# Hybrid decoder step: the rows of u and of v are fetched by two gathers in two layouts

## The chip, the cores and the metric

The kernel runs on one core of a Trainium2 chip, as one program. The metric is the device time of one execution in microseconds (us); a run's figure is the median of its executions. Five engines work beside each other and meet at semaphores: PE (TensorE, matrix products), DVE (VectorE), ACT (ScalarE), POOL (GpSimd) and SP (SyncE, which here only issues DMAs). Indirect DMAs, which fetch rows by a list of indices, are issued by POOL.

## The reference

One layer: a mixer (convolution and gated linear attention), then PEER, a retrieval of single-neuron experts. Only PEER is touched by the change. It runs over 1088 tokens (1024 of a prompt and 64 of samples):

```python
s = einsum('thpd,hpkd->thpk', (h @ wq), subkeys)       # 8 heads, 2 halves, 128 keys
sv, si = top_k(s, 16)
cand, cand_id = 16 x 16 sums of the two halves, ids si0 * 128 + si1
top_v, top_i = top_k(cand, 16)                         # 8 heads x 16 = 128 picks of a token
expert = cand_id[top_i]; gate = softmax(top_v)
act = gelu(einsum('thkd,td->thk', u_tab[expert], h))   # u_tab: 16384 x 1024
out = einsum('thk,thkd->td', gate * act, v_tab[expert])  # v_tab: 16384 x 1024
```

Each token picks 128 experts. For every pick a row of u (4 KB in float32) is needed for the dot product with the token's h, and a row of v (4 KB) is added to the token's output with the weight gate * gelu(dot).

## The kernel before

The program is a row of phases, one after the other: conditioning, attention heads, convolution, gates, merge, output projection, keys (which writes the lists `best` and `place`), then `gather_phase` (PEER proper) and `final_phase` (last norm and residual). The change is in `gather_phase` alone, and in `arrange`, which lays out the tables.

`gather_phase` takes the tokens in nine tiles: eight of 128 tokens and one of 64 (`NT`, `rows`). In each tile it goes token by token, in the order of `token_order` (column c of each of four groups of 32 tokens, then the next column), and makes batches of four tokens (`BT`).

- **POOL** issues one indirect DMA for each token (L1361). The 128 partitions hold the 128 picks of that token, the table `uv` has u and v side by side, so each of the 128 rows is 8 KB and a DMA brings 1 MB. There are `NUV` = 11 buffers of 1 MB. Before a DMA, POOL waits until the v product of the batch that used the buffer has been done (`v_mm`).
- **PE** spreads the token's h over all 128 partitions (`spread`, L1402: two products of 96 x 512 in bf16, h being held as three bf16 pieces, selected by `sel`), two tokens ahead at most (PSUM banks 0 to 3). It also makes the weighted sum of v rows (`gathered`, L1416), one batch behind: for each token two float32 products with a weight column `zw` into banks 4 and 5.
- **DVE** multiplies the token's u rows by the spread h and adds up along the row (L1632, one custom instruction with a u buffer in SBUF and the spread h in PSUM as its inputs), then, once per batch, makes gate * gelu in `weigh` (L1611). Four times in a tile it does a part of the next tile's choice of experts (`pick`, L1555 to L1592).
- **ACT** does gelu once per batch (L1529), cuts h into its bf16 pieces (L1470 to L1479), copies the turned h out of PSUM (L1487), and takes the finished tile out of PSUM and back (`emptied`, `returned`).
- **SP** loads h of the next tile and stores the output of the last.

The order on each engine is written out by hand in these loops. Waits are semaphores; an engine works its instructions strictly in the order in which they stand, so whatever stands behind a waiting instruction waits too. The lines that the change touches:

## Time and profile before

| | |
|---|---|
| median of 3 runs | 4817.19 us (4813.33 to 4823.47) |
| the profiled execution's own time | 4813.56 us |
| its span | 4811.8 us |
| first to last indirect DMA of `gather_phase` | 1883.91 to 4723.17 us, 1088 of them |
| busy share of the span: PE, DVE, POOL, ACT | 68%, 49%, 29%, 11% |
| queue of the indirect DMAs | 1140.92 MB, 57.5% of the 16 DMA engines' time over the whole span |

A span is the time from the first to the last instruction of the profiled execution; what lies around it is 1.8 us. A line of a profile view names the kernel's line, the engine, the operation, what is written <- what is read, shapes, count; then busy time, mean duration in ns, and the idle time that the engine had just before such instructions with who ended it. The share in which the 16 DMA engines are busy, and what they move, is a line of its own. "PEclk" is TensorE's granted clock as a share of its full speed.

### The profile page before, as it was taken

How to read it: one execution, taken by the hardware profiler on the slowest of the kernel's cores; microseconds unless marked ns; L12 is line 12 of the kernel's file. 1: busy time of each engine (PE TensorE's matmuls, PEld its weight loads, DVE VectorE, ACT ScalarE, POOL GpSimd, SP SyncE). 2: the span in 40 equal slices, each digit the busy share in tenths (PEclk: the TensorE clock that was granted, in tenths of full speed). 3: DMA queues.
4: the chain of work that ended last, by engine and by line, in shares of the span. 5: the costliest groups of instructions: out<-in, count | busy, mean ns of one | idle time of the engine just before them, and what ended most of it. 6: DMA issues, size and time to landing. Idle time of an engine off the chain costs nothing. (4 is left out here: it accounts for less than half of the span.)

```text
span 4811.8 us, 43674 instructions
## 1 busy us (share of the span) xinstructions
PE 3292.1 (68%) x15775; PEld 1751.6 (36%) x15775; DVE 2358.9 (49%) x5057; ACT 551.5 (11%) x999; POOL 1412.9 (29%) x1297
## 2 busy tenths in 40 slices
PE   8688996988984992566665665565665666655674
PEld 2577885988983990111111111111111111111111
DVE  0355335300314676655555555556546555556543
ACT  1222222011013111000000000000000000000001
POOL 0311100222311111343433333433333434333330
PEclk9899998999997995666666666666666766666687
DMA  6110111022321104999999999999999999999996
GB/s 247 48 46 27 46 38 55 26 95 111 124 87 77 54 22 183 396 392 410 409 388 409 393 405 408 385 422 401 388 421 405 391 406 411 390 406 411 417 422 251
DMA packets 206836, 1302.03 MB, mean 271 GB/s; under 512 B 25537, under 2 KB 42561, under 8 KB 61266
## 3 DMA queue, kind: packets, MB, share of 16 engines
q0 software_dynamic: 156672, 1140.92, 57.5%
q1 hardware_dynamic: 47554, 140.09, 8.0%
q10 hardware_dynamic: 2448, 18.88, 1.0%
q8 instruction: 100, 1.64, 0.1%
q14 instruction: 62, 0.51, 0.0%
HBM read 1259.27 MB, written 40.54 MB: 270 GB/s over the span
## 5 line engine op out<-in xcount | busy, mean ns | idle before, releaser
L1632 DVE CUSTOM_DVE_ANT_0 peer_uv<-peer_uv,all_PS 128x1024 f32<-128x1024 f32 x1088 | 1313.1, 1220 | 1245.7 <-PE all_PS L1402 694.7
L1361 POOL DMA_INDIRECT peer_uv<-in_uv,peer_idx x1088 | 1052.6, 967 | 1778.9 <-PE all_PS L1416 1493.0
L1416 PE MATMUL all_PS<-peer_uv,peer_zw 128*32 128x512 f32 x4352 | 947.8, 982 | 583.7 <-DVE peer_zw L1611 579.2
L1402 PE MATMUL all_PS<-peer_hT,peer_sel 96*128 96x512 bf16 x2176 | 770.2, 467 | 441.5 <-DVE peer_dots L1632 439.7
L1402 PEld LDWEIGHTS all_PS<-peer_hT,peer_sel 96*128 96x128 bf16 x2176 | 167.3, 107 | 1245.5 <-DVE peer_dots L1632 759.8
L1416 PEld LDWEIGHTS all_PS<-peer_uv,peer_zw 128*32 128x32 f32 x4352 | 165.3, 152 | 1136.2 <-DVE peer_zw L1611 762.8
L1529 ACT ACTIVATE peer_ge<-peer_dots 128x4 f32<-128x4 f32 x272 | 56.1, 206 | 2631.6 <-DVE peer_dots L1632 2626.7
L124 PE MATMUL all_PS<-stream_h_hi,keys_w_hi 128*128 128x384 f32 (+1 forms) x384 | 127.2, 331 | 60.3 <-DVE keys_w_lo L1239 51.4
L133 POOL CAST gla_w_hi<-gla_w 128x1024 fp32r<-128x1024 f32 x24 | 27.7, 1153 | 426.6 <-DMA gla_w<-in_w_heads 273.5
L124 PE MATMUL all_PS<-stream_h_hi,side_w_hi 128*128 128x384 f32 (+1 forms) x384 | 126.4, 329 | 16.8 <-DVE side_w_lo L771 16.8
L124 PE MATMUL all_PS<-stream_h_hi,gla_w_hi 128*128 128x384 f32 (+1 forms) x384 | 126.0, 328 | 1.8 <-DVE gla_low L641 1.8
L125 PE MATMUL all_PS<-stream_h_lo,side_w_hi 128*128 128x384 f32 (+1 forms) x384 | 126.2, 329 | 0.0
L126 PE MATMUL all_PS<-stream_h_hi,side_w_lo 128*128 128x384 f32 (+1 forms) x384 | 126.2, 329 | 0.0
L126 PE MATMUL all_PS<-stream_h_hi,keys_w_lo 128*128 128x384 f32 (+1 forms) x384 | 126.1, 328 | 0.0
L125 PE MATMUL all_PS<-stream_h_lo,keys_w_hi 128*128 128x384 f32 (+1 forms) x384 | 126.1, 328 | 0.0
L126 PE MATMUL all_PS<-stream_h_hi,gla_w_lo 128*128 128x384 f32 (+1 forms) x384 | 125.2, 326 | 0.0
L125 PE MATMUL all_PS<-stream_h_lo,gla_w_hi 128*128 128x384 f32 (+1 forms) x384 | 125.1, 326 | 0.0
L124 PE MATMUL all_PS<-stream_h_hi,conv_w_hi 128*128 128x384 f32 (+1 forms) x288 | 95.7, 332 | 23.8 <-DVE conv_w_lo L771 23.8
L771 DVE TENSOR_TENSOR merge_w_lo<-merge_w,merge_w_hi 128x512 fp32r<-128x512 f32 (+1 forms) x2 | 1.9, 958 | 201.3 <-ACT merge_w_hi L764 201.3
L124 PEld LDWEIGHTS all_PS<-stream_h_hi,keys_w_hi 128*128 128x128 f32 x384 | 72.9, 190 | 62.5 <-issue 51.9
L125 PE MATMUL all_PS<-stream_h_lo,conv_w_hi 128*128 128x384 f32 (+1 forms) x288 | 95.6, 332 | 0.0
L126 PE MATMUL all_PS<-stream_h_hi,conv_w_lo 128*128 128x384 f32 (+1 forms) x288 | 95.5, 331 | 0.0
(293 smaller groups left out, 4960.7 us busy)
## 6 DMA issues: line engine op xcount, KB each, us to landing
cond_w<-in_w_ada SPq DMA_DIRECT2D x12, 2048.0 KB, 7.7
peer_uv<-in_uv,peer_idx POOLq DMA_INDIRECT x1088
gla_w<-in_w_heads SPq DMA_DIRECT2D x24, 512.0 KB, 3.3
scratch_sig<-side_sig ACTq DMA_DIRECT2D x8, 1088.0 KB, 4.0
merge_sig<-scratch_sig ACTq DMA_DIRECT2D x8, 1088.0 KB, 5.0
side_w<-in_w_gate_ab SPq DMA_DIRECT2D x16, 512.0 KB, 3.2
keys_w<-in_w_query SPq DMA_DIRECT2D x16, 512.0 KB, 3.2
conv_w<-in_w_conv SPq DMA_DIRECT2D x12, 512.0 KB, 3.2
```

Of the source, the lines that this page charges most:

```text
L124: nc.tensor.matmul(bank[:, 0:n], w_hi[:, k, :], hi, start=(k == 0), stop=False)
L125: nc.tensor.matmul(bank[:, 0:n], w_hi[:, k, :], lo, start=False, stop=False)
L126: last = nc.tensor.matmul(bank[:, 0:n], w_lo[:, k, :], hi, start=False, stop=(k == nk - 1))
L133: nc.gpsimd.tensor_copy(hi, raw).then_inc(high, 1)
L771: nc.vector.tensor_tensor(self.lo[:, b, 0:nk], self.raw[:, b, 0:nk], self.hi[:, b, 0:nk].bitcast(F32), ALU.subtract).then_inc(self.low, 1)
L1361: nc.gpsimd.indirect_dma_start(out=uv[:, n % NUV, :], out_offset=None, in_=A["uv"], in_offset=bass.IndirectOffsetOnAxis(ap=idx[:, t % 2, r ...
L1402: last = nc.tensor.matmul(PS[:, 2 * (n % 2) + e, :], sel[:, c, :], hT[:, t % 2, j, e * 512:(e + 1) * 512], start=True, stop=True)
L1416: last = nc.tensor.matmul(PS[j * GR:(j + 1) * GR, 4 + e, :], zw[:, z, GR - 1 - c:2 * GR - 1 - c], uv[:, n % NUV, D + e * 512:D + (e + 1) * ...
L1529: nc.scalar.activation(ge[:, n % ND, :], dots[:, n % ND, :], ACT.Gelu_apprx_tanh).then_inc(M["gelled"], 1)
L1632: nc.vector.tensor_tensor_reduce(u, u, PS[:, 2 * (n % 2):2 * (n % 2) + 2, :].rearrange("p b d -> p (b d)"), 1.0, 0.0, ALU.mult, ALU.add, d ...
```

## The change

The table `uv` is split into `u` and `v`, and each has a gather, buffers and a layout of its own. A u gather now brings one pick of all 128 tokens of a tile: tokens stand on the partitions, rows are 4 KB, a DMA brings 0.5 MB (0.25 MB in the tile of 64 tokens). There are 128 of them in each of the nine tiles, 1152 in all. A v gather brings the 128 picks of one token, as before, but 4 KB a row; there are 1088. POOL issues them in turn, the u gather of tile t and then a v gather of tile t - 1. There are 8 buffers for u and 12 for v, of 0.5 MB each.

As u has tokens on the partitions, h need not be spread: DVE multiplies a u buffer by `hT`, the turned h of the tile, in SBUF. The spreading products, the bf16 pieces, the selection matrix and POOL's two subtractions in a tile are gone. Gelu and the weights are made once in a tile, from all 128 x 128 dots, and turned by PE; ACT then copies four columns of weights into `zw` for each batch. The index list is now made by DVE in the layout of the tokens (`idx`), turned by PE and copied by DVE for v (`idxT`).

```diff
-        NUV, NZ, ND, BT = 11, 3, 4, 4
-        uv = sc.sb("uv", [P, NUV, 2 * D])
+        NU, NV, NZ, BT = 8, 12, 3, 4
+        u, v = sc.sb("u", [P, NU, D]), sc.sb("v", [P, NV, D])
...
         @block.gpsimd
-                for i, (c, j) in enumerate(order[t]):
-                    n = before[t] + i
-                    if n >= NUV:
-                        pool.wait_ge(M["v_mm"], (n - NUV) // BT + 1)
-                    nc.gpsimd.indirect_dma_start(out=uv[:, n % NUV, :], out_offset=None, in_=A["uv"],
-                                                 in_offset=bass.IndirectOffsetOnAxis(ap=idx[:, t % 2, row(c, j):row(c, j) + 1], axis=0)
-                                                 ).then_inc(uv_in[n % NUV], 16)
+            def fetch_u(t, s):
+                n = HK * t + s
+                if n >= NU:
+                    pool.wait_ge(M["dotted"], n - NU + 1)
+                nc.gpsimd.indirect_dma_start(out=u[0:rows(t), n % NU, :], out_offset=None, in_=A["u"],
+                                             in_offset=bass.IndirectOffsetOnAxis(ap=idx[0:rows(t), t % 2, s:s + 1], axis=0)
+                                             ).then_inc(u_in[n % NU], 16)
+            def fetch_v(t, i):
+                c, j = order[t][i]
+                n = before[t] + i
+                if n >= NV:
+                    pool.wait_ge(M["v_mm"], (n - NV) // BT + 1)
+                nc.gpsimd.indirect_dma_start(out=v[:, n % NV, :], out_offset=None, in_=A["v"],
+                                             in_offset=bass.IndirectOffsetOnAxis(ap=idxT[:, t % 3, row(c, j):row(c, j) + 1], axis=0)
+                                             ).then_inc(v_in[n % NV], 16)
+            for t in range(NT + 1):
+                if t < NT:
+                    pool.wait_ge(M["idx_set"], t + 1)
+                    pool.wait_ge(M["n_set"], t + 1)
+                for n in range(P):
+                    if t < NT:
+                        fetch_u(t, n)
+                    if t and n < len(order[t - 1]):
+                        fetch_v(t - 1, n)
...
         @block.tensor
-                for e in range(2):
-                    last = nc.tensor.matmul(PS[:, 2 * (n % 2) + e, :], sel[:, c, :], hT[:, t % 2, j, e * 512:(e + 1) * 512],
-                                            start=True, stop=True)
-                last.then_inc(M["spread"], 1)
...
-                pe.wait_ge(M["weighed"], batches[t] + q + 1)
+                pe.wait_ge(M["spread"], batches[t] + q + 1)
...
+                        if e == 0:
+                            pe.wait_ge(v_in[n % NV], 16 * (n // NV) + 16)
...
         @block.scalar
+            def gelu(t):
+                act.wait_ge(M["dotted"], HK * (t + 1))
+                act.wait_ge(M["weighed"], t)
+                nc.scalar.activation(ge[0:m, :], dots[0:m, t % 2, :], ACT.Gelu_apprx_tanh).then_inc(M["gelled"], 1)
+            def spread(t, q):
...
+                nc.scalar.activation(zw[:, z:z + BT, GR - 1].rearrange("p (c j) -> p c j", c=cs),
+                                     wT[:, t % 2, 0:rows(t)].rearrange("p (j c) -> p c j", c=GR)[:, c:c + cs, :],
+                                     ACT.Copy).then_inc(M["spread"], 1)
...
         @block.vector
-                        dve.wait_ge(uv_in[n % NUV], 16 * (n // NUV) + 16)
-                        dve.wait_ge(M["spread"], n + 1)
...
-                        nc.vector.tensor_tensor_reduce(u, u, PS[:, 2 * (n % 2):2 * (n % 2) + 2, :].rearrange("p b d -> p (b d)"),
-                                                       1.0, 0.0, ALU.mult, ALU.add, dots[:, d, e:e + 1]).then_inc(M["dotted"], 1)
+                for s in range(HK):
+                    n = HK * t + s
+                    if s == 0:
+                        dve.wait_ge(M["h_out"], 2 * t + 2)
+                    dve.wait_ge(u_in[n % NU], 16 * (n // NU) + 16)
+                    nc.vector.tensor_tensor_reduce(u[0:m, n % NU, :], u[0:m, n % NU, :], hT[0:m, t % 2, :],
+                                                   1.0, 0.0, ALU.mult, ALU.add, dots[0:m, t % 2, s:s + 1]).then_inc(M["dotted"], 1)
+                    if s == 1 and t:
+                        weigh(t - 1)
+                    if t + 1 < NT:
+                        if s in (12, 28, 44, 60):
+                            pick(t + 1, (s - 12) // 16, step)
+                        if s == 104:
+                            named(t + 1)
```

How instructions move on the engines. On POOL, at the start of the phase (peer_uv are the 11 buffers, in_uv is the table, a count behind x says how many stand in a row), before:

```order
L1337 MEMSET peer_zw 128x756
L1343 TENSOR_TENSOR peer_second<-peer_h,peer_first 128x1024
L1350 TENSOR_TENSOR peer_hp<-peer_second,peer_third 128x32x32
L1361 DMA peer_uv<-in_uv,peer_idx 128x2048 x45
L1343 TENSOR_TENSOR peer_second<-peer_h,peer_first 128x1024
```

and with the change, the same place:

```order
L1336 MEMSET peer_zw 128x756
L1343 DMA peer_u<-in_u,peer_idx 128x1024 x129
L1353 DMA peer_v<-in_v,peer_idxT 128x1024
L1343 DMA peer_u<-in_u,peer_idx 128x1024
L1353 DMA peer_v<-in_v,peer_idxT 128x1024
L1343 DMA peer_u<-in_u,peer_idx 128x1024
```

The first tile has 128 u gathers and nothing else; from the second on, u and v gathers alternate, two DMAs of half the size where one stood.

On DVE, where the dots of the first tile begin, before (the second row of each pair reads the accumulated sum):

```order
L1598 SCALAR_TENSOR_TENSOR peer_idx<-peer_routeT 128x128
L1632 ISA peer_uv,peer_dots<-peer_uv,all_PS 128x1024
L1632 ISA peer_dots 128x1
L1632 ISA peer_uv,peer_dots<-peer_uv,all_PS 128x1024
L1632 ISA peer_dots 128x1
```

and with the change:

```order
L1564 SCALAR_TENSOR_TENSOR peer_expert<-peer_pair 128x128
L1566 CAST peer_idx<-peer_expert 128x128
L1574 CAST peer_idxT<-all_PS 128x128
L1597 ISA peer_u,peer_dots<-peer_u,peer_hT 128x1024
L1597 ISA peer_dots 128x1
L1597 ISA peer_u,peer_dots<-peer_u,peer_hT 128x1024
L1597 ISA peer_dots 128x1
```

The second input of the dots has moved from PSUM (all_PS) to SBUF (peer_hT).

On PE, in the first tile of before:

```order
L1402 MATMUL all_PS<-peer_hT,peer_sel 128x512 x8
L1416 MATMUL all_PS<-peer_uv,peer_zw 32x512 x8
L1402 MATMUL all_PS<-peer_hT,peer_sel 128x512 x8
L1416 MATMUL all_PS<-peer_uv,peer_zw 32x512 x8
```

and with the change, in the second round of the loop, which is the first with v rows:

```order
L1403 MATMUL all_PS<-peer_v,peer_zw 32x512 x72
L1374 MATMUL all_PS<-all_ident,peer_h 128x128 x4
L1403 MATMUL all_PS<-peer_v,peer_zw 32x512 x16
L1374 MATMUL all_PS<-all_ident,peer_h 128x128 x4
L1403 MATMUL all_PS<-peer_v,peer_zw 32x512 x112
```

The spreading is gone, and what is left between the v products is the turning of the next tile's h.

## Rows read from the trace of the kernel before

**Rows 1.** The page's 40 slices: DMA share in tenths, and GB/s.
```profile
DMA  6110111022321104999999999999999999999996
GB/s 247 48 46 27 46 38 55 26 95 111 124 87 77 54 22 183 396 392 410 409 388 409 393 405 408 385 422 401 388 421 405 391 406 411 390 406 411 417 422 251
```
**Rows 2.** Stretches: the whole gather, and one tile (stretch, length, busy of engines, PEclk, DMA share, GB/s).
```profile
1883.90:4723.20 2839.30, 1739.05 (x6842) 371.00 (x6843) 1591.60 (x3074) 166.46 (x426) 1083.93 (x1104) 0.68 0.98 404
2219.40:2554.90 335.50, 203.29 (x807) 43.20 (x803) 189.02 (x366) 20.29 (x51) 128.66 (x130) 0.67 0.98 401
```
**Rows 3.** Waits, 1900 to 4620 us.
```profile
POOL peer_uv L1361 <- PE all_PS L1416: 1435.0, 257, 16.9
DVE peer_uv L1632 <- PE all_PS L1402: 645.9, 247, 5.7
```
**Rows 4.** Timeline, POOL: first, second and last indirect DMA (start, duration).
```profile
1883.91 1.11 POOL L1361 DMA_INDIRECT peer_uv<-in_uv,peer_idx  x1 [23.87 <-DVE peer_idx L1598]
1885.33 0.94 POOL L1361 DMA_INDIRECT peer_uv<-in_uv,peer_idx  x1 [0.30 <-issue]
1886.58 0.94 POOL L1361 DMA_INDIRECT peer_uv<-in_uv,peer_idx  x1 [0.30 <-issue]
...
4723.17 0.94 POOL L1361 DMA_INDIRECT peer_uv<-in_uv,peer_idx  x1 [5.28 <-PE all_PS L1416]
```
**Rows 5.** Tile peer_uv: duration in ns of POOL's DMAs and DVE's dots, min/median/max.
```profile
L1361 POOL DMA_INDIRECT peer_uv<-in_uv,peer_idx x1088: 935/941/2682, 1883.9 to 4723.2; - x182
L1632 DVE CUSTOM_DVE_ANT_0 peer_uv<-peer_uv,all_PS x1088: 1207/1221/1223, 1894.4 to 4733.6; 128x1024 f32<-128x1024 f32 x182
```
**Rows 6.** Timeline, DVE: two dots back to back.
```profile
1948.36 1.22 DVE L1632 CUSTOM_DVE_ANT_0 peer_uv<-peer_uv,all_PS 128x1024 f32<-128x1024 f32 x1
1949.50 1.22 DVE L1632 CUSTOM_DVE_ANT_0 peer_uv<-peer_uv,all_PS 128x1024 f32<-128x1024 f32 x1
```
**Rows 7.** Timeline, POOL and DVE, around the third part of a pick.
```profile
2371.75 2.67 POOL L1361 DMA_INDIRECT peer_uv<-in_uv,peer_idx  x1 [0.30 <-issue]
...
2371.32 2.29 DVE L1581 TENSOR_TENSOR peer_sums<-peer_halff,all_iota 128x2048 f32<-128x2048 f32 x1
2373.64 2.29 DVE L1584 TENSOR_TENSOR peer_sums<-peer_sums,peer_place 128x2048 f32<-128x2048 f32 x1
```
**Rows 8.** The same, around the first part of another pick.
```profile
2264.14 0.94 POOL L1361 DMA_INDIRECT peer_uv<-in_uv,peer_idx  x1 [0.30 <-issue]
2264.30 2.29 DVE L1555 TENSOR_TENSOR peer_sums<-peer_best 128x2048 f32<-128x2048 f32 x1
2265.38 2.02 POOL L1361 DMA_INDIRECT peer_uv<-in_uv,peer_idx  x1 [0.30 <-issue]
```
**Rows 9.** Timeline, DVE: first and last instruction of pick parts 1 and 4.
```profile
1929.39 2.29 DVE L1555 TENSOR_TENSOR peer_sums<-peer_best 128x2048 f32<-128x2048 f32 x1
1940.66 0.41 DVE L1563 MATCH_REPLACE8 peer_sums<-peer_top,peer_sums 128x256 f32<-128x256 f32 x1
2092.83 2.29 DVE L1581 TENSOR_TENSOR peer_sums<-peer_halff,all_iota 128x2048 f32<-128x2048 f32 x1
2100.36 0.29 DVE L1592 TENSOR_TENSOR peer_route<-peer_diff,peer_total 128x128 f32<-128x128 f32 x1
```
**Rows 10.** DMA queues (packets, MB, share of 16 engines), and the load of w_heads.
```profile
q0 software_dynamic: 156672, 1140.92, 57.5%
q1 hardware_dynamic: 47554, 140.09, 8.0%
gla_w<-in_w_heads SPq DMA_DIRECT2D x24, 512.0 KB, 3.3
```
**Rows 11.** Stretches, as in rows 2: the program's start, and the gather's first full load.
```profile
0.00:60.00 60.00, 50.06 (x129) 12.55 (x130) 1.17 (x6) 7.97 (x11) 1.10 (x10) 1.00 0.89 355
1894.00:1914.00 20.00, 14.30 (x51) 2.50 (x49) 12.28 (x22) 0.88 (x3) 6.58 (x7) 0.59 1.01 424
```
**Rows 12.** Timeline, PE: the last batch of v products.
```profile
4735.29 5.32 PE L1416 MATMUL all_PS<-peer_uv,peer_zw 128*32 128x512 f32 x16 [3.19 <-DVE peer_zw L1611]
```

More of the change, by code:

```diff
@@ new lines, in turn, with names_turned @@
+                pe.wait_ge(M["h_out"], 2 * (t - 1) + e + 1 if t else 0)
+                for k in range(KD // 2):
+                    last = nc.tensor.transpose(PS[0:m, e, k * P:(k + 1) * P], h[:, e * KD // 2 + k, 0:m], G["ident"][:, :])
+                last.then_inc(M["h_mm"], 1)
+            def names_turned(t):
+                m = rows(t)
+                pe.wait_ge(M["own"], OPS * t + OPS)
+                pe.wait_ge(M["n_set"], t)
+                nc.tensor.transpose(PS[:, 6, 0:m], expert[0:m, :], G["ident"][0:m, 0:m]).then_inc(M["n_mm"], 1)
@@ L1432, in _ @@
-            pe.wait_ge(M["ready"], 2)
-            routes(0)
-            turn(0)
-            pe.wait_ge(M["x_out"], 2 * 4)
-            for t in tiles:
-                for q in range(per[t]):
-                    spread(t, BT * q)
-                    spread(t, BT * q + 1)
-                    if q:
-                        gathered(t, q - 1)
-                    elif t:
-                        gathered(t - 1, per[t - 1] - 1)
-                    spread(t, BT * q + 2)
-                    spread(t, BT * q + 3)
-                    if q == 2 and t:
-                        back(t - 1)
-                    if t + 1 < NT:
-                        if q == 16:
-                            turn(t + 1)
-                        if q == 26:
-                            routes(t + 1)
-                        if q == per[t] - 1:
-                            pe.wait_ge(M["x_out"], 2 * (4 * (t + 1) + rows(t + 1) // GR))
@@ L1455, in _ @@
-            gathered(NT - 1, per[NT - 1] - 1)
-            back(NT - 1)
+                pe.wait_ge(M["yT_out"], 2 * (t - 1) + e + 1 if t else 0)
+                for k in range(KD // 2):
+                    last = nc.tensor.transpose(PS[:, (3, 7)[e], k * P:k * P + m], y[0:m, (e * 4 + k) * P:(e * 4 + k + 1) * P],
+                                               G["ident"][0:m, 0:m])
+                last.then_inc(M["y_mm"], 1)
+            names_turned(0)
+            for e in range(2):
+                turn(0, e)
@@ new lines, in _ @@
+            for t in range(NT + 1):
+                for q in range(NB):
+                    if t and q == 0:
+                        weights_turned(t - 1)
+                    if t and q < per[t - 1]:
+                        gathered(t - 1, q)
+                    if t > 1 and q in (2, 3):
+                        back(t - 2, q - 2)
+                    if t + 1 < NT:
+                        if q in (8, 10):
+                            turn(t + 1, (q - 8) // 2)
+                        if q == 24:
+                            names_turned(t + 1)
@@ L1458, in _, with turned @@
+            for e in range(2):
+                back(NT - 1, e)
         @block.scalar
         def _(act):
-            act.wait_ge(M["sel_landed"], 16)
-            nc.scalar.activation(sel[:], sel_in[:, :, None].broadcast_to([3 * GR, GR, P]), ACT.Copy).then_inc(M["ready"], 1)
-            nc.scalar.activation(ident[:, :], G["ident"][:, :], ACT.Copy).then_inc(M["ready"], 1)
-            def pieces(t):
+            def turned(t, e):
                 m = rows(t)
-                act.wait_ge(M["h_in"], 16 * t + 16)
-                if t:
-                    act.wait_ge(M["x_mm"], 8 * t)
-                nc.scalar.activation(first[:, :, 0:m], h[:, :, 0:m], ACT.Copy)
-                nc.scalar.activation(hp[:, :, 0:m // GR, 0, :], h[:, :, 0:m].rearrange("p k (j c) -> p k j c", c=GR),
-                                     ACT.Copy).then_inc(M["h_one"], 1)
@@ new lines, in returned @@
+                if t and e == 0:
+                    act.wait_ge(M["y_saved"], 16 * t)
+                nc.scalar.activation(yT[:, 4 * e:4 * e + 4, 0:m],
+                                     PS[:, (3, 7)[e], :].rearrange("p (k t) -> p k t", k=4)[:, :, 0:m], ACT.Copy).then_inc(M["yT_out"], 1)
+            act.wait_ge(M["zeros"], 1)
+            soft(0)
+            for e in range(2):
+                turned(0, e)
+            for t in range(NT + 1):
+                if t:
+                    gelu(t - 1)
+                    weights(t - 1)
+                    if t > 1:
+                        emptied(t - 2)
+                for q in range(NB):
+                    if t and q < per[t - 1]:
+                        spread(t - 1, q)
+                    if t > 1 and q in (3, 4):
+                        returned(t - 2, q - 3)
+                    if t + 1 < NT:
+                        if q in (9, 11):
+                            turned(t + 1, (q - 9) // 2)
+                        if q == 14:
```

234 lines of the change are left out of this document (72 added, 162 removed).

## The prediction

> **What bounds the kernel now.** I read the 40 slices first: from slice 17 on, six tenths of the span, the DMA share stands at 9 tenths, at about 400 GB/s [rows 1]. Everything before and after that is untouched by the change. The stretch from the first to the last indirect DMA is 2839.3 us [rows 2, 4] and holds 8.5 tiles, so 334 us a tile; one tile read alone shows a DMA share of 0.98 at 401 GB/s, with PE at 203, DVE at 189 and POOL at 129 of 335.5 us [rows 2]. The waits say the same: POOL waited 1435 us for v products to free a buffer, and DVE 646 us for spread h, but with all transfers queued behind one another that idle time is the effect of a full DMA queue [rows 3]. So the DMA engines bound this stage. They have to move 1140.9 MB before and after [rows 10]: 1088 x 1 MB before, 8 x 128 x 0.5 + 128 x 0.25 + 1088 x 0.5 MB after, the same. What is taken from PE (L1402) is not on the path.
>
> The second engine to watch is POOL. Back to back its DMAs start 1.25 us apart (0.94 busy, 0.30 between) [rows 4]. A tile now asks for 128 of them, 160 us; after the change it asks for 256, 256 x 1.245 = 319 us, against 334 of the DMA engines. In a pair of one u and one v gather: POOL 2.49 us, DMA 334/128 = 2.61 us. The slack is 0.12 us a pair.
>
> **What may eat the slack.** The 1088 DMAs of POOL have a median of 941 ns and a longest of 2682 [rows 5]. In the whole trace 21 are longer than 2 us. Each of them starts while DVE is in a TENSOR_TENSOR with both inputs in SBUF (L1555, L1581, L1584), and each ends 0.8 us after that instruction: 2371.75 + 2.67 = 2374.42, and L1581 ends at 2373.61; L1584, which follows at once, doesn't hold it again [rows 7]. In the other example 2265.38 + 2.02 = 2267.40 against the end of L1555 at 2266.59, while the DMA that began 0.16 us before L1555 took its 0.94 [rows 8]. No DMA that starts inside such an instruction escapes. So the issue needs something about 0.14 us after its start that DVE holds for the length of such an instruction, and then 0.8 us more. The dots of before, with one input in PSUM, never do this: 1088 of 1.22 us fill half of the stage [rows 5] and the median issue is untouched. After the change the dots have both inputs in SBUF, and there are 1152.
>
> The Trainium skill, SBUF — State Buffer, section Who interferes with whom, states this as a rule: a DVE instruction with two SBUF inputs contends with a GpSimd instruction that reads SBUF, since they share a read interface, as an exclusive lock; the trace agrees, in 21 of 21. 
>
> **The change part by part**, from the first indirect DMA (1883.9 us) on, against 2839.3 us.
>
> 1. *First tile, u alone.* Moves half of a tile's bytes: DMA 167 us, POOL 128 x 1.245 = 159, DVE 128 x 1.14 [rows 6] = 146 plus the four pick parts. These last 11.7 us (the first), 7.8 (the last) [rows 9], and 7 each for the two between by their kin; sum 34. DVE: 180 us. So DVE bounds here, not DMA, and with eight u buffers, 8 x 1.3 = 10 us of DMA, the picks are not quite hidden. Low 180; with every issue and dot getting in each other's way, 230; taken 200, nearer the low end, as 1.245 is longer than a dot of 1.14 and issues can fall between dots.
>
> 2. *Seven tiles with u and v.* Low end: the DMA pace of before, 7 x 335.5 = 2349. High end by chance phase: a dot holds for 1.14 us once in a pair of length C, so an issue meets one with chance 1.14/C and then waits 0.57 on average, twice in a pair: C = 2.49 + 2 x (1.14/C) x 0.57, so C = 2.93 and a tile is 375 us. Worse is a lock in which the v issue is held for some 0.7 us in every pair, C = 3.19, 408 us. But phase is not chance. A dot starts when its u lands, a fixed time after its issue. An issue of at least 0.94 + 3.3 us (the load of 512 KB with 4 KB rows lands in 3.3 us [rows 10]) puts the dot's end some 5.2 us behind the moment at which its issue read the list, two cycles of 2.6: it falls on the next u issue's moment and holds it little. And as long as DMA is the slower one, a delay up to 0.12 us a pair is free. The two-cycle lock is undone after each pick, when DVE works off a backlog back to back: 34/2.61 = 13 dots a tile, 15 us, some 12 issues each of which may wait up to 1.04 us more: 12 us, half of it taken, 6 us. I take C = 2.70, a third of the way from 2.61 to 2.93: 128 x 2.70 + 6 = 352 us, times seven 2464.
>
> 3. *Ninth tile of 64 tokens with the v of the eighth.* DMA has only 128 x (0.65 + 1.30) = 250 us, so POOL bounds: 128 x 2.49 = 319 us without any hold, 375 by chance phase; no slack of DMA hides anything. No pick stands in it. Taken 350. (If issues of 64 rows are shorter in proportion, 29 us less: in the low end.)
>
> 4. *Last round, 64 v gathers:* 64 x 1.30 = 83 us.
>
> 5. *Row size.* 4 KB rows instead of 8 KB, so twice the packets. The program's start moves rows of 2 KB and 4.25 KB (by the code, w_ada and x) at 355/0.89 = 399 GB/s of a full share, against 401/0.98 = 409 in the gather [rows 2, 11]; taken nothing, high end in the third rival.
>
> 6. *All else.* The spreading products (part of PE's 203 us a tile), ACT's pieces and POOL's two subtractions a tile go; all lay beside the DMA, gain 0. v products: 5.3 us for a batch of four [rows 12], and even twice that is about the 10.4 us which four pairs give, so PE keeps up at a lower granted clock too. Gelu, weights and their turn come once in a tile with 12 v buffers, 31 us, before POOL is stopped; the chain is a few instructions of under 1 us: 0. The next index list is ready at dot 104 of 128, with up to 8 u gathers run ahead: 0. The start and the end of the stage: the first dot began 10.5 us after the first DMA [rows 4, 5], while the queue filled anyway, and the last batch is alike: 0.
>
> Sum: 200 + 2464 + 350 + 83 = 3097, against 2839: +258. Own time 4813.6 + 258 = 5072; against the median, 3.6 us higher, it is the same within what I claim. Forecast 5070 us.
>
> **Rivals.**
>
> *The dots don't hold POOL* (the custom instruction is not a TENSOR_TENSOR, and no row shows it with two SBUF inputs). Then 180 + 2349 + 319 + 83 = 2931, +92: 4905 us, or 4876 with the shorter issues of 64 rows. The first tile, which uses half the queue, and the ninth, bound by POOL, remain. For it: only TENSOR_TENSOR was seen. Against it: the two differ in nothing else that the rows show. Chance 0.20.
>
> *Chance phase or worse.* 200 + 7 x (375 + 6) + 375 + 83 = 3325, +486: 5299 us; at C = 3.19 with 12 us after picks, 230 + 7 x 420 + 375 + 83 = 3628, +789: 5602. For it: a landing varies by more than 0.1 us, so a lock may not hold. Chance 0.20.
>
> *Small rows are slow.* The indirect queue spent 282.6 ns a packet of 7282 bytes in the mean, the plain queue 129.5 ns for 2946 bytes (57.5% and 8.0% of 16 x 4811.8 us over their packets [rows 10]). A line through them gives 154 ns for the 3641 bytes that a mean packet would have (8 of 9 are rows of 4 KB), so 308 ns for what took 283: 9% more. A pair is then 2.84, and 190 + 7 x 364 + 319 + 90 = 3147, +308: 5121 us, with POOL's holds hidden below it. Against it: the 399 GB/s above. Chance 0.10.
>
> *Faster: the DMA engines run nearer their peak.* Before, each gather of 1 MB waited for four buffers to come free together, and the rate was 401 to 404 GB/s; just after the start, with all buffers free, it was 424 GB/s at a share of 1.01 [rows 11]. If the finer buffers kept that up, a pair would take 2.47 us, POOL's 2.49 would rule, and 180 + 7 x 319 + 290 + 80 = 2783, -56: 4757 us. It decides from a pair below (2839 - 180 - 319 - 83)/896 = 2.52 us on, and asks that no dot holds POOL at all. The share of 0.98 leaves 2% only. Chance 0.03.
>
> **How the numbers follow.** Forecast 0.45 (with its own range 4960 to 5200), the rivals 0.20, 0.20, 0.10 and 0.03, and 0.02 that gains and losses meet within 0.2%, about what a measurement of this kernel can tell from no change. Faster 0.03, same 0.02, slower 0.95. The range reaches from 4880, the case without holds, to 5310, chance phase; what is worse is left out.
>
> **What would show it.** POOL's DMAs: 2240, with a mean well above today's 941 ns median and many between 0.95 and 2.1 us, each slow one ending 0.8 us after a dot. If their mean stays at 0.94, the holds are wrong; if their idle time still is a wait for v products or dots and the DMA share is 0.98, POOL isn't the bound. The first tile should last about 200 us, the seven about 350 each with a DMA share near 0.93, the ninth about 350 with a share near 0.7. A u dot should last 1.2 us still. PE's busy share in the stage should fall below half. The forecast is wrong if a tile with u and v stays at 335 us, or if DVE's dots, not POOL's issues, become longer.

## The result and the profile after

The changed kernel takes 5313.02 us (median of 4 runs, 5295.60 to 5318.75) against 4815.26 us before (4 runs): a ratio of 1.103, 95% interval 1.100 to 1.106. The forecast of 5070 us had the direction, but half of the size: 258 us against 498. The range ended at 5310.

The page of the profiled execution (5295.6 us, span 5293.8), the lines that answer to [rows 1] and [rows 10]:

```profile
DMA  5111001124221168999999999999999999999996
GB/s 225 52 42 50 26 25 66 70 92 140 78 91 37 51 216 324 360 362 365 351 358 372 351 361 369 361 377 369 342 372 349 365 359 352 365 337 268 241 283 266
...
q0 software_dynamic: 314368, 1140.99, 60.0%
```

The same 1141 MB, with a DMA share of 9 tenths as before, but at 360 GB/s where it was 404. Two packets stand where one stood. A packet took 60.0% x 16 x 5293.8 / 314368 = 161.7 ns in the mean, so two of them 323, where one of twice the size took 283.

The costliest groups of POOL and DVE on the page (line, engine, what is written <- read, count; busy us, mean ns; idle before and who ended it):

```profile
L1597 DVE CUSTOM_DVE_ANT_0 peer_u<-peer_u,peer_hT 128x1024 f32<-128x1024 f32 (+1 forms) x1152 | 1399.3, 1224 | 1524.9 <-DMA peer_u<-in_u,peer_idx 1369.5
L1343 POOL DMA_INDIRECT peer_u<-in_u,peer_idx x1152 | 1260.3, 1094 | 438.1 <-issue 392.9
L1353 POOL DMA_INDIRECT peer_v<-in_v,peer_idxT x1088 | 1253.1, 1152 | 423.6 <-issue 324.5
```

and the gathers by tile, with their durations in ns (min/median/max), which answer to [rows 5]:

```profile
L1343 POOL DMA_INDIRECT peer_u<-in_u,peer_idx x1152: 895/941/3032, 1886.0 to 5117.4; - x192
L1353 POOL DMA_INDIRECT peer_v<-in_v,peer_idxT x1088: 935/955/2026, 2106.3 to 5214.6; - x182
```

An issue now takes 1.09 and 1.15 us in the mean, and the dots as long as ever. DVE no longer waits for spread h but for u rows.

Stretches of the stage (length, busy of PE, PEld, DVE, ACT, POOL, PEclk, DMA share, GB/s): the first tile, one of the seven with u and v, the ninth, and the last round. They answer to [rows 2].

```profile
1886.00:2105.00 219.00, 2.44 (x9) 1.75 (x9) 182.74 (x329) 2.79 (x4) 162.99 (x128) 0.50 0.85 305
2853.10:3229.20 376.10, 215.94 (x532) 33.46 (x532) 190.76 (x341) 12.35 (x42) 284.18 (x256) 0.73 0.96 361
4728.10:5117.40 389.30, 238.34 (x505) 33.22 (x505) 152.33 (x249) 8.77 (x37) 311.89 (x255) 0.66 1.03 256
5117.40:5214.60 97.20, 80.84 (x269) 16.84 (x267) 7.64 (x13) 5.34 (x21) 63.67 (x65) 0.95 0.99 359
```

The reader should see two suspects in the second row. POOL is busy 284 us, and with the 0.30 us that each of its 256 issues has in front of it that is 361 of 376 us. The DMA engines are busy too, 0.96, at a rate 11% below the 404 GB/s of before. The last row is nearly without dots (DVE is busy 7.6 us in it), and still 64 gathers of 0.5 MB took 97 us, 1.52 us each where I had put 1.30.

How a hold looks now, on POOL's timeline behind a part of a pick (start, duration):

```profile
2911.10 0.94 POOL L1353 DMA_INDIRECT peer_v<-in_v,peer_idxT  x1 [0.30 <-issue]
2916.90 1.69 POOL L1343 DMA_INDIRECT peer_u<-in_u,peer_idx  x1 [4.86 <-DVE peer_dots L1597]
2918.89 1.98 POOL L1353 DMA_INDIRECT peer_v<-in_v,peer_idxT  x1 [0.30 <-issue]
2921.18 1.99 POOL L1343 DMA_INDIRECT peer_u<-in_u,peer_idx  x1 [0.30 <-issue]
2923.47 1.99 POOL L1353 DMA_INDIRECT peer_v<-in_v,peer_idxT  x1 [0.30 <-issue]
2925.76 0.94 POOL L1343 DMA_INDIRECT peer_u<-in_u,peer_idx  x1 [0.30 <-issue]
```

and DVE's in the same stretch:

```profile
2918.84 1.22 DVE L1597 CUSTOM_DVE_ANT_0 peer_u<-peer_u,peer_hT 128x1024 f32<-128x1024 f32 x1
2919.99 1.22 DVE L1597 CUSTOM_DVE_ANT_0 peer_u<-peer_u,peer_hT 128x1024 f32<-128x1024 f32 x1
2921.13 1.22 DVE L1597 CUSTOM_DVE_ANT_0 peer_u<-peer_u,peer_hT 128x1024 f32<-128x1024 f32 x1
```

DVE works off its backlog back to back, a dot every 1.14 us, and an issue gets through once in two dots: 2918.89, 2921.18 and 2923.47 are 2.29 us apart instead of 1.24. The issue of 2918.89 began 0.05 us after a dot; that dot ended about 2920.06, and the issue 0.81 us later, at 2920.87. So the custom instruction does hold POOL. In the whole trace 565 of the 2240 issues are longer than 1.15 us; they end 0.81 us (median) after the end of a dot or of a TENSOR_TENSOR.

Two theories were therefore tested, R (4 KB rows cost the DMA engines more per byte) and H (dots hold POOL's issues).

### The profile page after: what moved, and what is told of

Same layout as the page of the kernel before. It is cut to its first block and busy times, and to the rows that moved or that the text cites. A ratio compares the mean times of both kernels' runs of the same rounds, so it can differ in the third digit from the quotient of the medians.

```text
span 5293.8 us, 38526 instructions
## 1 busy us (share of the span) xinstructions
PE 3449.7 (65%) x13390; PEld 1669.2 (32%) x13390; DVE 2438.3 (46%) x4940; ACT 478.3 (9%) x918; POOL 2837.1 (54%) x2431
## 3 DMA queue, kind: packets, MB, share of 16 engines
q0 software_dynamic: 314368, 1140.99, 60.0%
## 5 line engine op out<-in xcount | busy, mean ns | idle before, releaser
L1403 PE MATMUL all_PS<-peer_v,peer_zw 128*32 128x512 f32 x4352 | 1879.9, 903 | 1181.7 <-DMA peer_v<-in_v,peer_idxT 1011.4
L1597 DVE CUSTOM_DVE_ANT_0 peer_u<-peer_u,peer_hT 128x1024 f32<-128x1024 f32 (+1 forms) x1152 | 1399.3, 1224 | 1524.9 <-DMA peer_u<-in_u,peer_idx 1369.5
L1343 POOL DMA_INDIRECT peer_u<-in_u,peer_idx x1152 | 1260.3, 1094 | 438.1 <-issue 392.9
L1353 POOL DMA_INDIRECT peer_v<-in_v,peer_idxT x1088 | 1253.1, 1152 | 423.6 <-issue 324.5
L1403 PEld LDWEIGHTS all_PS<-peer_v,peer_zw 128*32 128x32 f32 x4352 | 272.1, 134 | 2732.8 <-DMA peer_v<-in_v,peer_idxT 1869.7
L1474 ACT ACTIVATE peer_zw<-peer_wT 128x4 f32<-128x4 f32 x272 | 51.9, 209 | 2135.3 <-PE all_PS L1403 943.4
L133 POOL CAST side_w_hi<-side_w 128x1024 fp32r<-128x1024 f32 x14 | 14.5, 1037 | 170.1 <-PE all_PS L126 170.1
L133 POOL CAST keys_w_hi<-keys_w 128x1024 fp32r<-128x1024 f32 x14 | 14.5, 1039 | 168.6 <-ACTq L1227 168.6
```

Of the source, the lines that this page charges most:

```text
L133: nc.gpsimd.tensor_copy(hi, raw).then_inc(high, 1)
L1343: nc.gpsimd.indirect_dma_start(out=u[0:rows(t), n % NU, :], out_offset=None, in_=A["u"], in_offset=bass.IndirectOffsetOnAxis(ap=idx[0:rows ...
L1353: nc.gpsimd.indirect_dma_start(out=v[:, n % NV, :], out_offset=None, in_=A["v"], in_offset=bass.IndirectOffsetOnAxis(ap=idxT[:, t % 3, row ...
L1403: last = nc.tensor.matmul(PS[j * GR:(j + 1) * GR, 4 + e, :], zw[:, z, GR - 1 - c:2 * GR - 1 - c], v[:, n % NV, e * 512:(e + 1) * 512], sta ...
L1474: nc.scalar.activation(zw[:, z:z + BT, GR - 1].rearrange("p (c j) -> p c j", c=cs), wT[:, t % 2, 0:rows(t)].rearrange("p (j c) -> p c j", ...
L1597: nc.vector.tensor_tensor_reduce(u[0:m, n % NU, :], u[0:m, n % NU, :], hT[0:m, t % 2, :], 1.0, 0.0, ALU.mult, ALU.add, dots[0:m, t % 2, s: ...
```

## The experiments

Each ratio is against the kernel before, timed in the same group (4817, 4821 and 4824 us in the three groups); the ratios' intervals are within 0.005 of the ratio, that of the 8 KB rows 0.011. The changed kernel itself was timed in another group, with 4815 us before.

**1. No dot with two inputs in SBUF.**

```diff
-                    last = nc.tensor.transpose(PS[0:m, e, k * P:(k + 1) * P], h[:, e * KD // 2 + k, 0:m], G["ident"][:, :])
+                    last = nc.tensor.transpose(PS[0:m, 2 * (t % 2) + e, k * P:(k + 1) * P], h[:, e * KD // 2 + k, 0:m], G["ident"][:, :])
...
-            for e in range(2):
-                turned(0, e)
...
-                        if q in (9, 11):
-                            turned(t + 1, (q - 9) // 2)
...
-                        dve.wait_ge(M["h_out"], 2 * t + 2)
+                        dve.wait_ge(M["h_mm"], 2 * t + 2)
...
-                    nc.vector.tensor_tensor_reduce(u[0:m, n % NU, :], u[0:m, n % NU, :], hT[0:m, t % 2, :],
+                    nc.vector.tensor_tensor_reduce(u[0:m, n % NU, :], u[0:m, n % NU, :],
+                                                   PS[0:m, 2 * (t % 2):2 * (t % 2) + 2, :].rearrange("p b d -> p (b d)"),
```

`turned` was ACT's copy of the turned h out of PSUM; it is no longer called.

> The changed kernel, but the dots read the turned h from PSUM (four banks, two per tile), so that no dot has two inputs in SBUF; all DMAs, rows and waits of the gathers stay. Theory H (dots hold POOL's issues, which sets the pace): every issue back at 0.94 us, a tile with u and v falls from 374 us to 319-335, the whole to 4880-4950 us. Theory R (gathers of 4 KB rows move only 359 to 376 GB/s of a full DMA share, so the DMA engines set the pace and the holds hide below them): the issues are 0.94 us too, but a tile stays at 358-374 us and the whole at 5150-5300 us, with POOL idle in front of its gathers.

Measured: 5199.92 us, ratio 1.079 (1.077 to 1.082), 113 us less than the changed kernel. The u gathers' durations:

```profile
L1343 POOL DMA_INDIRECT peer_u<-in_u,peer_idx x1152: 891/937/2741, 1888.9 to 5014.2; - x192
```

and three stretches, a middle tile, the ninth, the last round:

```profile
2807.20:3170.80 363.60, 218.12 (x530) 34.19 (x530) 189.42 (x340) 11.37 (x40) 245.01 (x256) 0.75 0.96 372
4638.50:5014.20 375.70, 229.73 (x493) 31.95 (x491) 149.18 (x245) 8.74 (x37) 234.32 (x255) 0.68 1.03 260
5014.20:5119.40 105.20, 85.03 (x279) 16.76 (x279) 10.05 (x17) 5.31 (x21) 60.90 (x66) 0.92 1.00 352
```

The issues are short again (40 of 2240 take over 1.0 us, those beside the picks), POOL is 45 us short of filling a tile (256 x 1.245 = 319 of 364), and the tile still takes 364 us. So the holds are worth the 113 us, and something else most of the rest. Theory R says that it is the DMA engines. Their mean rate, 372 GB/s, looks like it, but a mean over a tile hides two states. Two stretches inside that tile:

```profile
2900.00:2930.00 30.00, 17.41 (x46) 2.72 (x48) 19.68 (x50) 0.21 (x1) 22.68 (x25) 0.81 1.03 409
2937.50:2940.00 2.50, 1.47 (x6) 0.50 (x10) 1.23 (x2) 0.42 (x2) 0.94 (x1) 0.50 0.30 121
```

While the queue is full, rows of 4 KB move at 409 GB/s: 2.56 us a pair, 328 us a tile, less than the 335.5 us of a tile before. Then the queue runs dry, because POOL has stopped:

```profile
2932.06 0.94 POOL L1343 DMA_INDIRECT peer_u<-in_u,peer_idx  x1 [0.31 <-issue]
2938.91 0.94 POOL L1353 DMA_INDIRECT peer_v<-in_v,peer_idxT  x1 [5.91 <-remote]
```

That gather needs the count of finished v batches (`v_mm`) of the batch that used its buffer. By PE's rows that batch had ended 19 us earlier, and ACT, which needs the same count for its next weights, went on at the same moment as POOL:

```profile
2917.47 2.59 PE L1403 MATMUL all_PS<-peer_v,peer_zw 128*32 128x512 f32 x10 [0.65 <-issue]
2938.67 0.21 ACT L1474 ACTIVATE peer_zw<-peer_wT 128x4 f32<-128x4 f32 x1 [21.62 <-remote]
```

"remote" means that the profile names nobody who ended the wait. In the kernel before, POOL goes on 0.3 us after the batch that it waits for; here the pauses come mostly once in 32 gathers (45 us) and end 17 us (median) after it. POOL's time in the seven middle tiles adds up, in us:

| | h in PSUM | changed |
|---|---|---|
| 1792 issues, one each 1.2425 us | 2227 | 2227 |
| what longer issues have above 0.94 us | 47 (34 issues) | 282 (583 issues) |
| pauses, what they have above 0.30 us | 282 (59 pauses) | 103 (28 pauses) |
| sum | 2556 | 2612 |
| measured | 2555 | 2623 |

So POOL sets the pace of the seven tiles in both kernels, and the DMA engines wait for it. Theory H is shown. Of theory R the pace is there and the reason is not. Why the count comes late is open.

**2. 4 KB rows in the kernel before.**

```diff
-                    nc.gpsimd.indirect_dma_start(out=uv[:, n % NUV, :], out_offset=None, in_=A["uv"],
+                    for e, name in enumerate(("u", "v")):
+                        nc.gpsimd.indirect_dma_start(out=uv[:, n % NUV, e * D:(e + 1) * D], out_offset=None, in_=A[name],
```

> The kernel before with one edit: each token's gather is issued as two, u and v from tables of their own, so rows are 4 KB and POOL issues 256 DMAs a tile; the dots still read h from PSUM, so nothing holds POOL. Theory H: POOL needs 319 us a tile, less than the 334 of the DMA engines, so the time stays within 4810-4860 us. Theory R: a tile goes from 334 to 358-374 us and the whole to 5000-5150 us.

Measured: 5325.73 us, ratio 1.106 (1.103 to 1.109): slower than R allowed. A tile took 398 us, the DMA engines busy 0.90 at 339 GB/s. H alone (4810 to 4860) is refuted. POOL's pauses are here too, 3.2 us after 16 gathers in the stretches between picks:

```profile
2967.46 0.94 POOL L1362 DMA_INDIRECT peer_uv<-in_v,peer_idx  x1 [0.30 <-issue]
2971.60 0.94 POOL L1362 DMA_INDIRECT peer_uv<-in_u,peer_idx  x1 [3.19 <-DMA cond_x<-in_x]
```

The buffer's batch had ended 5.4 us before, and the name of the releaser can't be right: `cond_x` belongs to a phase that is long over. Where the queue is full, 4 KB rows move at 412 GB/s in this run as well.

**3. The same with a list of consecutive rows.**

```diff
-                                                 in_offset=bass.IndirectOffsetOnAxis(ap=idx[:, t % 2, row(c, j):row(c, j) + 1], axis=0)
+                                                 in_offset=bass.IndirectOffsetOnAxis(ap=seq[:, i:i + 1], axis=0)
```

Here seq[p, i] = 128 * i + p.

> As the kernel before with each gather split into two of 4 KB rows, but with a list of consecutive row numbers in place of the chosen experts, so that each DMA reads 512 KB in one piece (experts other than the chosen ones are used). If 4 KB rows are slow because they lie scattered in memory, it is faster than the same kernel with the chosen rows and near 4815 us; if the price is one per row, it equals it. Under theory H both are near 4815-4860 us.

Measured: 5315.73 us, ratio 1.104 (1.101 to 1.107), the same as experiment 2. It is not that the rows lie scattered in memory. As POOL's pauses take part in setting the pace of both runs, a small effect on the DMA engines could hide below them.

**4. The same as experiment 2 with 13 buffers.**

```diff
-        NUV, NZ, ND, BT = 11, 3, 4, 4
+        NUV, NZ, ND, BT = 13, 3, 4, 4
```

> The kernel before with each gather split into two of 4 KB rows, with 13 buffers in place of 11. With 11 it took 5326 us, a tile 398 us, the DMA engines busy 0.90 at 340 GB/s and POOL 0.64. If that was the want of buffers (POOL needs 10 us for the eight gathers of four freed buffers, so the queue of the DMA engines runs dry), a tile falls to 360-370 us with a share of 0.97, and the whole to 5000-5090 us. If 4 KB rows cost that much by themselves, it stays at 5326.

Measured: 5336.54 us, ratio 1.106 (1.104 to 1.109), a tile 398 us. My explanation by a want of buffers is wrong. A clean stretch between two picks of this trace has 16 issues of POOL and a pause of 3.4 us in 23 us, so 2.88 us a token and 369 us a tile, near the pace of experiment 1 and made in the same way: 16 x 1.2425 + 3.4 = 23.3, with the buffer's batch mostly 4 to 8 us old. The other 30 us a tile come in pauses of 8 to 9 us in front of gathers whose buffer had just come free (0.3 us). What delays those batches I have not settled.

**5. Holds without small rows.** The kernel before, its dots reading a constant tile in SBUF, so they leave h out.

```diff
-                        nc.vector.tensor_tensor_reduce(u, u, PS[:, 2 * (n % 2):2 * (n % 2) + 2, :].rearrange("p b d -> p (b d)"),
+                        nc.vector.tensor_tensor_reduce(u, u, hs[:, :],
```

> The kernel before with one edit: the dots take their second input from a constant tile in SBUF instead of the spread h in PSUM (so the dots are not those of the reference), all waits kept. Holds without 4 KB rows. Theory H: POOL's 1088 DMAs get longer, from a mean of 0.97 to some 1.2 us, each long one ending 0.8 us after a dot; as POOL has half its time to spare the whole stays within 4810-4860 us. Theory R says nothing on the issues and also 4815 us. If the custom instruction does not hold POOL, the mean stays at 0.97.

Measured: 4851.06 us, ratio 1.007 (1.005 to 1.010), and the issues:

```profile
L1363 POOL DMA_INDIRECT peer_uv<-in_uv,peer_idx x1082 | 1318.6, 1219 | 1505.7 <-PE all_PS L1418 1245.5 <-issue 259.3
```

From 0.97 us to 1.22: the holds come with the SBUF input and cost 0.7% even where POOL has half its time to spare. The 446 issues above 1.15 us end 0.81 us (median) after a dot or a TENSOR_TENSOR.

**6. Shorter holds.** The changed kernel, dots over half of the elements.

```diff
-                    nc.vector.tensor_tensor_reduce(u[0:m, n % NU, :], u[0:m, n % NU, :], hT[0:m, t % 2, :],
+                    nc.vector.tensor_tensor_reduce(u[0:m, n % NU, 0:D // 2], u[0:m, n % NU, 0:D // 2], hT[0:m, t % 2, 0:D // 2],
```

> The changed kernel with dots over 512 of 1024 elements (both inputs still in SBUF, half of each sum left out): DVE holds POOL for 0.57 us in place of 1.14. By chance phase POOL's pair is C = 2.49 + 2 x (0.6/C) x 0.3, so 2.62 us, below the 2.85 us of the DMA engines (365 us a tile): holds then cost nothing in the seven tiles, and the whole falls from 5313 to 5190-5220 us, that of h in PSUM. If something else about the two inputs in SBUF cost the 113 us, it stays near 5300.

Measured: 5211.31 us, ratio 1.079 (1.074 to 1.083), a tile 366 us, as with h in PSUM. Shorter dots take the holds away as PSUM does. The floor under them is again POOL's: longer issues fall to 91 us in the seven tiles, and the pauses are back at 235.

**7. Twice the holds.** The changed kernel with each dot run a second time.

```diff
+                    nc.vector.tensor_tensor_reduce(scr[0:m, n % 2, :], u[0:m, n % NU, :], hT[0:m, t % 2, :],
+                                                   1.0, 0.0, ALU.mult, ALU.add, junk[0:m, n % 2:n % 2 + 1]).then_inc(twice, 1)
                     nc.vector.tensor_tensor_reduce(u[0:m, n % NU, :], u[0:m, n % NU, :], hT[0:m, t % 2, :],
```

> The changed kernel with each dot run twice (the first to a scratch tile): DVE has 190 of 374 us of work a tile, so 340 after. By chance phase, with POOL let in between two dots, C = 2.49 + 2 x (2.28/C) x 0.57, so 3.27 us, 418 us a tile: whole 5600-5750 us. If the holds did not bound the changed kernel in any part, the time moves less than 1%, except in the first tile, where DVE's work becomes 128 x 2.3 + 34 = 328 us (+110 us): about 5420. If POOL is not let in between, 5800 or more.

Measured: 5543.31 us, ratio 1.151 (1.148 to 1.154), 230 us more than the changed kernel. First tile and a middle one:

```profile
1888.60:2206.90 318.30, 2.44 (x9) 1.75 (x9) 312.34 (x567) 2.79 (x4) 213.06 (x128) 0.50 0.70 213
...
3000.10:3392.70 392.60, 230.36 (x531) 34.80 (x530) 336.59 (x597) 12.33 (x42) 301.76 (x256) 0.70 0.94 345
```

The middle tile grew from 375 to 394 us in the mean of seven, not to 418. POOL fills it: 302 us busy and 256 x 0.30 between issues are 379 of the 392.6 us above. In the seven tiles its longer issues grew from 282 to 466 us and its pauses fell from 103 to 59. So the holds bound it, but chance phase overrates them: 3.08 us a pair against 3.27 worked out. That issues settle between dots more often than by chance is my reading, not shown.

**8. 8 KB rows in the changed layout.** Experiment 1, but each gather brings the whole row of u and v from one table.

```diff
-        NU, NV, NZ, BT = 8, 12, 3, 4
+        NU, NV, NZ, BT = 6, 8, 3, 4
...
-                nc.gpsimd.indirect_dma_start(out=u[0:rows(t), n % NU, :], out_offset=None, in_=A["u"],
+                nc.gpsimd.indirect_dma_start(out=u[0:rows(t), n % NU, :], out_offset=None, in_=A["uv"],
```

> The changed kernel with h in PSUM, but each gather of u and of v fetches the whole row of 8 KB from one table and uses its half (6 and 8 buffers of 1 MB), so twice the bytes, the same number of DMAs and packets of twice the size. If the price is one per packet, a pair takes what two gathers of before took, 2 x 2.61 us, 668 us a tile, and the whole about 1884 + 335 + 7 x 668 + 668 + 167 + 80 = 7810 us. If it lies in anything but the row size (the two layouts, the order, POOL), bytes go on at the rate of 4 KB rows: a pair 5.7 us, a tile 730 us and the whole about 8350 us.

Measured: 7780.24 us (runs from 7689 to 7841), ratio 1.603 (1.593 to 1.614), where 7810 and 8350 had been set against each other. A stretch of 30 us, the seven middle tiles, and the ninth:

```profile
2900.00:2930.00 30.00, 13.79 (x24) 2.19 (x24) 15.32 (x45) 0.69 (x2) 12.29 (x13) 0.56 1.01 421
2207.00:6682.00 4475.00, 1984.45 (x3674) 258.02 (x3674) 1333.98 (x2373) 79.64 (x277) 1727.73 (x1793) 0.55 1.01 421
6682.00:7509.40 827.40, 289.29 (x519) 35.58 (x519) 155.31 (x255) 8.74 (x37) 234.22 (x254) 0.54 1.01 243
```

A tile takes 639 us, not the 668 expected, and the ninth 827: that the sum came out near 7810 is luck. The queue is full throughout, at 421 GB/s. Against the mean of experiment 1, 372, a byte would cost 13% more in rows of 4 KB. But that mean holds POOL's pauses; full queue against full queue it is 409 to 421, 3%. My test could not tell the two apart: with 1 MB a gather POOL has work for 319 of 639 us, so a limit of POOL's would vanish as well as one of the row size. No pause of the kind of experiment 1 is in this trace.

**9. The ninth tile.** Experiment 1, the last tile's u gathers with 128 rows to 128 partitions.

```diff
-                nc.gpsimd.indirect_dma_start(out=u[0:rows(t), n % NU, :], out_offset=None, in_=A["u"],
-                                             in_offset=bass.IndirectOffsetOnAxis(ap=idx[0:rows(t), t % 2, s:s + 1], axis=0)
+                lst = min(t, NT - 2)
+                nc.gpsimd.indirect_dma_start(out=u[:, n % NU, :], out_offset=None, in_=A["u"],
+                                             in_offset=bass.IndirectOffsetOnAxis(ap=idx[:, lst % 2, s:s + 1], axis=0)
```

> As the changed kernel with h in PSUM (5200 us, ninth tile 376 us, moving 260 GB/s), but the u gathers of the ninth tile fetch 128 rows to all 128 partitions by the eighth tile's list, 32 MB more (the last tile's dots are those of other experts). If a gather to 64 partitions costs the DMA engines as much time as one to 128, the ninth tile becomes like the others, 360-376 us, and the whole stays within 5185-5205 us. If it costs by bytes or rows, the 64-row gathers were not the bound in that tile, and it grows by up to 128 x 0.7 = 90 us, to 5230-5290 us.

Measured: 5190.18 us, ratio 1.077 (1.075 to 1.078): 32 MB more and not slower. The ninth tile:

```profile
4659.50:5020.00 360.50, 220.17 (x521) 32.67 (x519) 155.29 (x255) 8.44 (x37) 237.97 (x255) 0.74 0.96 372
```

It is a tile like the others, at 372 GB/s; with 64 rows it moved 260 in 376 us, with the DMA engines busy 1.03 and POOL idle for 63 us more than between issues. A gather of 64 rows to 64 partitions costs the DMA engines at least as much as one of 128 to 128: at the rate of a full queue the v gather of a pair takes 1.28 us, which leaves 1.66 of the 2.94 for the u gather, an estimate from these rows. The edit changes rows and partitions together, so the run can't say which of them it is. The Trainium skill, SBUF — State Buffer, section Door 1: The DMA port swizzle, says that bandwidth depends on how many of the 16 ports the partitions reach, and that the second 64 partitions lie on the other half of them; the trace agrees in kind, 260 GB/s against 372 with the v gathers of full width in between.

**10. v rows alone,** one gather of 4 KB rows a token in the kernel before; dots and weighted sum both read them.

```diff
-                    nc.gpsimd.indirect_dma_start(out=uv[:, n % NUV, :], out_offset=None, in_=A["uv"],
+                    nc.gpsimd.indirect_dma_start(out=uv[:, n % NUV, D:2 * D], out_offset=None, in_=A["v"],
...
-                        u = uv[:, n % NUV, 0:D]
+                        u, su = uv[:, n % NUV, D:2 * D], scr[:, n % 2, :]
...
-                        nc.vector.tensor_tensor_reduce(u, u, PS[:, 2 * (n % 2):2 * (n % 2) + 2, :].rearrange("p b d -> p (b d)"),
+                        nc.vector.tensor_tensor_reduce(su, u, PS[:, 2 * (n % 2):2 * (n % 2) + 2, :].rearrange("p b d -> p (b d)"),
```

> The kernel before with gathers of v rows alone, 4 KB in place of 8, one DMA a token (dots and weighted sum both read the v rows), so half the bytes and POOL needs only 160 us a tile. By bytes a tile would be 167 us of DMA, by packets of 155 ns 179; DVE has 190 us a tile, so DVE and its chain set the time, a tile 200-230 us, the whole 3650-3900 us. What it tells: the time of a packet where POOL has half its time to spare. Row price: 150-160 ns a packet in the queue's row; no row price: 141.

Measured: 4374.39 us, ratio 0.907 (0.906 to 0.909), a tile 283 us where I had put 200 to 230. The queue's packets and their share, and then a middle tile:

```profile
q0 software_dynamic: 156672, 570.49, 38.4%
```

```profile
2738.40:3021.70 283.30, 178.67 (x811) 40.74 (x811) 184.71 (x369) 20.24 (x51) 127.94 (x131) 0.76 0.72 241
```

With the DMA engines at 0.72 and DVE at 185 of 283 us, no engine is full, and I take it for the chain of the kernel before (spread, dot, gelu, weights, product), in which the engines wait for one another; that is argued, not tested. A packet took 171.5 ns, above the 150 to 160 that R gave; in a queue that runs empty between bursts this is no clean price. What the trace does tell: with rows of 4 KB but one gather a token, every pause for a v batch ends within 2 us of that batch. So the late counts don't come with small rows alone. They stand in the traces in which POOL issues two gathers of 4 KB back to back; that this is their cause is not shown.

**11. The kernel before with 13 buffers.**

```diff
-        NUV, NZ, ND, BT = 11, 3, 4, 4
+        NUV, NZ, ND, BT = 13, 3, 4, 4
```

> The kernel before with 13 buffers of 1 MB in place of 11. Its DMA share is 0.98 with 11; if the last 2% are a want of buffers at the picks, up to 2% of 2839 us are to be had, 4770-4815 us; if they are the engines' own, it stays at 4815.

Measured: 4746.98 us, ratio 0.984 (0.982 to 0.986). The line of GB/s by slices of the span, and then a middle tile, which takes 327 us:

```profile
GB/s 251 49 33 40 48 38 29 54 78 78 155 69 90 77 31 55 419 410 421 421 408 420 422 401 421 416 408 421 399 421 421 402 421 421 408 416 421 422 421 237
```

```profile
2528.60:2856.00 327.40, 191.59 (x812) 42.39 (x813) 189.31 (x370) 20.56 (x52) 129.99 (x130) 0.71 1.00 414
```

This beats both kernels. A DMA share of 0.98 still hid 1.6% of the whole time.

## Why the prediction was wrong, step by step

The stage by its parts, from first to last gather of the profiled executions, in us:

| part | before | forecast | forecast without holds | h in PSUM (no holds) | changed |
|---|---|---|---|---|---|
| first tile | | 200 | 180 | 195 | 219 |
| seven tiles | | 2464 | 2349 | 2555 | 2623 |
| ninth | | 350 | 319 | 376 | 389 |
| last round | | 83 | 83 | 105 | 97 |
| sum | 2839 | 3097 | 2931 | 3231 | 3329 |

- **What bounds the kernel**: right for the kernel before, with too small a margin: I took a share of 0.98 for a full queue; two more buffers gave 414 GB/s and 1.6% of the whole (experiment 11). For the changed kernel it is wrong in the seven tiles. POOL sets their pace, not the DMA engines.
- **Steps 2 and 6, a pair without holds at 2.61 us: this is the step that failed.** I gave POOL 2.49 us a pair, the DMA engines 2.61, and the wait for v products nothing ("so PE keeps up", 12 v buffers: 0). Without dots that hold, the seven tiles take 2555 us, 2.85 a pair, not 2349: POOL's 2.49, another 0.31 in pauses in front of v gathers, and 0.05 for issues held beside the picks (experiment 1). The slack of 0.12 us in which delays were to be free is POOL's own and was used up. In the changed kernel the pauses are 103 us of the seven tiles (79 of them in front of v gathers, 25 in front of u gathers that wait for dots behind a pick); forecast 2464, measured 2623.
- **Step 5, row size, "taken nothing"**: near enough. A full queue moves 4 KB rows at 409 GB/s and 8 KB rows at 421, so 3%; a pair needs 2.56 us of the DMA engines, below the 2.61 that I used. My 399 GB/s from plain loads was even lower. The rival "small rows are slow" gave 2.84 us a pair, and h in PSUM has 2.85: the number fits and its reason doesn't. It also took its price from a line through two queues, one of them of plain loads.
- **Step 3, the ninth tile:** I charged a gather to 64 partitions by its bytes, 0.65 us. It costs at least the time of a full one (experiment 9), and the DMA engines bound this tile at a share of 1.03: 376 us with h in PSUM against 319 of POOL. Holds matter little there: with half, whole and double dots it took 388, 389 and 389 us.
- **The holds** exist as foreseen: long issues end 0.8 us after a dot, an SBUF input alone brings them (experiments 1, 5), and they end with shorter dots (6). Their sum was put at 3097 - 2931 = 166 us; measured 98 in the profiles, 113 in the medians. By themselves they were not oversized: the longer issues of the seven tiles grew by 235 us with them, but POOL's pauses shrank by 179. The two costs take each other's place and don't add.
- **Step 1, the first tile:** 219 against 200, of which holds are 24; in it a dot starts as often as an issue.
- **The rival "chance phase"** gave 5299 us, close to the measured time, and for the wrong reason: it needs every microsecond to come from holds, and taking them away leaves 5200. A number that fits does not show its cause; experiment 7 shows chance phase too high as well. No rival had holds and a slower floor together.
- **PE, the index lists, the weights once in a tile**: no gain and no delay of their own that a run shows. The sign that PE's busy share would fall below half did not come: 216 of 376 us in the tile above.

Open: why the count of v batches reaches POOL and ACT up to 20 us late when POOL issues 4 KB gathers back to back, and why the kernel before with split gathers needs another 30 us a tile (experiments 2 to 4). The last round, 14 to 22 us above its 83, was not taken apart. More v buffers in the changed layout were not tried, nor fewer, larger gathers of 4 KB rows.

## What to carry to other kernels

Before splitting a gather, count the DMAs as well as the bytes: twice as many brought POOL from 129 of 335 us to nearly the whole tile, and every pause of POOL then costs time. Compare rates only where the queue is full in both kernels; a mean over a tile (372 GB/s) can look like a slower DMA (409 when full). Add up the bounding engine's time, issues, longer issues and pauses, before naming another. Keep operands of long VectorE instructions in PSUM when GpSimd issues indirect DMAs beside them, and give a DMA-bound loop a buffer more before believing that a share of 0.98 is full.

## What the runs showed of the hardware

- An indirect DMA of 128 rows costs GpSimd 0.94 us and 0.30 us between, for rows of 4 and of 8 KB alike; 64 rows cost 0.90 us. In these runs issue time goes with the number of DMAs and not with their bytes.
- A VectorE instruction with two SBUF inputs, the custom multiply-and-add included, holds an indirect DMA's issue until it ends; the issue then needs 0.8 us more. Behind a backlog of such instructions an issue gets through once in 2.29 us.
- Gathers of 128 rows to 128 partitions, queue full: 421 GB/s in rows of 8 KB, 409 GB/s in rows of 4 KB (experiments 1 and 8). Consecutive rows were no faster than scattered ones at 339 GB/s and a share of 0.90 (experiments 2 and 3).
- With 4 KB gathers issued back to back, two a token, POOL and ACT saw the count of finished v batches up to 20 us after PE's last product of the batch (experiment 1: pauses of 5.7 us in the median, mostly once in 32 gathers). With 8 KB rows (before, experiments 8 and 11) or one 4 KB gather a token (10) they did not. The cause is open.
- A gather of 64 rows to 64 partitions costs the DMA engines at least the time of one of 128 to 128: with the second one of a pair at full width, 260 against 372 GB/s, and 32 MB more took no longer.
